# Sums of weight blocks made in DRAM during the first layer's down product, and a later turn of the last group

## The reference

```
for l in range(2):
    x = x + mixers(rms_norm(x)) @ w_out[l]            # even layer: convolution + differential attention
    h = rms_norm(x, ffn_norm_w[l])                    # odd layer: gated DeltaNet + forgetting attention
    x = x + (silu(h @ w_gate[l]) * (h @ w_up[l])) @ w_down[l]
return rms_norm(x, final_norm_w)
```

## Time and profile before

| | |
|---|---|
| median of 3 runs | 1217.36 us (1217.2 to 1217.74) |
| the profiled execution | 1218.75 us |
| its span, first to last instruction | 1216.9 us |
| busy: TensorE, DVE, ACT, POOL | 1201.6, 784.4, 566.3, 107.1 us |
| accumulating DMAs (POOL's queue q0) | 6912 packets, 24.38 MB |

### The profile page before, as it was taken

How to read it: one execution, slowest core, us unless ns; L and a number is a source line. 1 busy time by engine, 2 the same in 40 slices (tenths; PEclk the granted TensorE clock), 3 DMA queues, 4 the chain that set the end, 5 groups by cost and what they waited for, 6 DMA issues and landing times.

```text
span 1216.9 us, 16112 instructions
## 1 busy us (share of the span) xinstructions
PE 1201.6 (99%) x5831; PEld 972.4 (80%) x5831; DVE 784.4 (64%) x1233; ACT 566.3 (47%) x917; POOL 107.1 (9%) x209
## 2 busy tenths in 40 slices
PE   9999999999999999999999999999999999999998
PEld 7876648888888878888888788788888888888876
DVE  6787886786667763337677666545665455456796
ACT  6354455655555543325585254444243232324564
POOL 0000000011110100000002814400000000000120
PEclk9999999999999999999999999999999999999999
DMA  6243311687867533331322211022244443336881
GB/s 247 90 118 91 106 54 52 225 189 174 210 174 187 108 100 91 100 104 55 119 87 70 87 35 53 18 61 66 83 134 116 116 109 104 93 104 223 167 147 70
DMA packets 56643, 138.04 MB, mean 113 GB/s; under 512 B 21890, under 2 KB 22146, under 8 KB 56322
## 3 DMA queue, kind: packets, MB, share of 16 engines
q1 hardware_dynamic: 48754, 111.44, 28.7%
q0 software_dynamic: 6912, 24.38, 11.4%
q10 hardware_dynamic: 912, 1.35, 0.4%
HBM read 128.61 MB, written 2.10 MB: 107 GB/s over the span
## 4 chain that ended last, share of the span: by engine, by line
PE 89%; DVE 5%; ACT 3%; issue 1%; DMA 1%; ACTq 0%; SPq 0%; DVEq 0%
PE PS L2168 87%; PE PS L2481 1%; DVE wring L1648 1%; DMA raw<-w_stream 1%; PE PS L2244 1%; DVE resid L1652 0%; DVE kept L1688 0%; DVE cacc L1843 0%; ACT wring L924 0%; ACTq L1194 0%; DVE wring L1698 0%; PE PS L2559 0%; DVE AA L1692 0%; DVE out L2159 0%; DVE amax L1761 0%
## 5 line engine op out<-in xcount | busy, mean ns | idle before, releaser
L2168 PE MATMUL PS<-HH,wring 128*128 128x512 f32 x2136 | 506.2, 393 | 0.9 <-DVE vd L2094 0.9
L2168 PEld LDWEIGHTS PS<-HH,wring 128*128 128x128 f32 x2136 | 395.2, 188 | 81.4 <-issue 1.3
L2168 PE MATMUL PS<-wring,HH 128*128 128x512 f32 x672 | 156.0, 390 | 0.3 <-ACT wring L1139 0.3
L2168 PEld LDWEIGHTS PS<-wring,HH 128*128 128x128 f32 x672 | 125.7, 188 | 26.6 <-issue 0.6
L1698 DVE TENSOR_TENSOR wring<-raw,wring 128x1024 fp32r<-128x1024 f32 x91 | 111.8, 1231 | 48.2 <-ACT wring L924 48.1
L924 ACT ACTIVATE wring<-raw 128x1024 fp32r<-128x1024 f32 x91 | 95.8, 1056 | 96.0 <-PE PS L2168 68.6
L2168 PE MATMUL PS<-AS,wring 128*128 128x512 f32 x528 | 120.4, 389 | 0.0
L2168 PEld LDWEIGHTS PS<-AS,wring 128*128 128x128 f32 x528 | 99.0, 188 | 20.5
L2168 PE MATMUL PS<-wring,AA 128*128 128x512 f32 x462 | 105.4, 389 | 1.6 <-DVE wring L1648 0.8
L2168 PEld LDWEIGHTS PS<-wring,AA 128*128 128x128 f32 x462 | 86.6, 188 | 20.3 <-issue 2.3
L1464 DVE TENSOR_TENSOR ubuf<-PS,rstd 128x512 f32<-128x512 f32 x22 | 15.2, 690 | 83.9 <-PE PS L2168 83.9
(11 more groups left out here) (367 smaller groups left out, 1606.1 us busy)
## 6 DMA issues: line engine op xcount, KB each, us to landing
raw<-w_stream SPq DMA_DIRECT2D x131, 512.0 KB, 3.5
x_even<-w_glu POOLq DMA_DIRECT2D x12, 512.0 KB, 6.3
raw<-w_glu SPq DMA_DIRECT2D x10, 512.0 KB, 9.4
y_part<-w_glu SPq DMA_DIRECT2D x10, 512.0 KB, 6.6
w_part<-w_glu SPq DMA_DIRECT2D x10, 512.0 KB, 5.3
w_part<-w_glu POOLq DMA_DIRECT2D x10, 512.0 KB, 10.9
kept<-w_last POOLq DMA_DIRECT2D x10, 512.0 KB, 8.3
x_odd<-w_glu POOLq DMA_DIRECT2D x8, 512.0 KB, 6.2
```

Source lines behind the costliest of these rows:

```text
L2168: return nc.tensor.matmul(out, lhsT, rhs, start=start, stop=stop, skip_group_check=adds)
```

## The change

```diff
+MADE_OF = {P_21: 0, P_SUM: 1, P_ALL: 2, P_LAST: 3}
+SUM_HALVES = 2
...
+    GROWN_BEFORE = [16 * len(range(n, GROWN_0, ADDING)) for n in range(ADDING)]
...
-        return more_tile(i) if a in (P_22, P_LAST) else kept_tile(i)
+        return more_tile(i) if a in (P_22, P_SUM, P_LAST) else kept_tile(i)
...
@@ SP, the last product
-        sp.dma_start(more_first[:], last_d[B22][:, 0:3 * TILE]).then_inc(first_loaded[0], 16)
-        sp.wait_ge(sem("ffn_lo"), SPLITS_0 + HALF)
-        sp.wait_ge(sem("lhs_made"), MADE)
-        sp.dma_start(more_last[:], last_d[B22][:, 3 * TILE:HALF * S]).then_inc(first_loaded[1], 16)
+        for i in range(PIECES):
+            if i == 3:
+                sp.wait_ge(sem("ffn_lo"), SPLITS_0 + HALF)
+                sp.wait_ge(sem("lhs_made"), MADE)
+            sp.dma_start(more_tile(i), last_d[B22][:, columns_of(i)]).then_inc(more_loaded[i], 16)
+        for a in (P_21, P_SUM, P_ALL, P_LAST):
+            if a == P_LAST:
+                sp.wait_ge(added[SUM_HALVES], GROWN_BEFORE[SUM_HALVES] + 32)
+            else:
+                for h in range(SUM_HALVES):
+                    sp.wait_ge(added[h], GROWN_BEFORE[h] + 16 * sums_in_dram(a))
+            for i in range(PIECES):
+                free = last_tile((a - 2) * PIECES + i)
+                sp.wait_ge(lo_ready[free % RING], slot_round(free))
+                if a in (P_21, P_ALL):
+                    sp.dma_start(kept_tile(i), sums_d[MADE_OF[a]][:, columns_of(i)]).then_inc(kept_loaded[i], 16)
+                else:
+                    sp.dma_start(more_tile(i), sums_d[MADE_OF[a]][:, columns_of(i)]).then_inc(more_loaded[i], 16)
@@ POOL, behind the accumulations of layer 0
+        pool.wait_ge(tile_used, T_DN0 + RING)
+
+        def grow(n, step, to, addend, columns, adds):
+
+            if step or GROWN_BEFORE[n]:
+                pool.wait_ge(added[n], GROWN_BEFORE[n] + 16 * step)
+            if adds:
+                nc.gpsimd.dma_start(to[:, columns], addend[:, columns], accum_op=ALU.add, max_dma_last_dim=5632).then_inc(added[n], 16)
+            else:
+                nc.gpsimd.dma_start(to[:, columns], addend[:, columns]).then_inc(added[n], 16)
+
+        first, second, third, fourth = sums_d[0], sums_d[1], sums_d[2], sums_d[3]
+        every = slice(0, HALF * S)
+        chain = ((first, last_d[B11], False), (first, last_d[B21], True), (second, first, False), (second, last_d[B22], True),
+                 (third, second, False), (third, last_d[B12], True))
+        for step, (to, addend, adds) in enumerate(chain):
+            for h in range(SUM_HALVES):
+                grow(h, step, to, addend, slice(h * HALF * S // 2, (h + 1) * HALF * S // 2), adds)
+            if step < 2:
+                grow(SUM_HALVES, step, fourth, last_d[(B21, B22)[step]], every, step == 1)
         pool.wait_ge(evacuated, E_IN1)
         nc.gpsimd.memset(cin[:, 0:GTAPS - 1], 0.0).then_inc(sem("cin_zero"), 1)
...
-        for a, part, behind in ((P_21, B21, P_11), (P_LAST, B21, P_21), (P_ALL, B12, P_SUM)):
-            for i in range(PIECES):
-                add_to_kept(a, i, part, behind)
@@ DVE, last_product
-                if g // PIECES == P_21:
-                    i = g % PIECES
-                    dve.wait_ge(first_loaded[i // 3], 32)
-                    dve.wait_ge(lo_ready[last_tile(g) % RING], slot_round(last_tile(g)))
-                    V.tensor_tensor(kept_tile(i), kept_tile(i), more_tile(i), ALU.add).then_inc(sem("lhs_made"), 1)
@@ TensorE, down
+            pe.wait_ge(sem("copied"), 4 * GROUPED)
+            columns(4, range(RING))
+            pe.wait_ge(sem("ffn_mul"), glu_made(GROUPED - 1, "gate_first", 1))
+            columns(0, (0, 1))
+            turn_results(GROUPED - 1, 0)
+            columns(0, (2, 3))
+            pe.wait_ge(sem("ffn_mul"), glu_made(GROUPED - 1, "up_second", 1))
+            columns(2, (0, 1))
+            turn_results(GROUPED - 1, 2)
+            columns(2, (2, 3))
+            pe.wait_ge(sem("glu_kept"), 4 * GROUPED)
+            columns(6, range(RING))
```

More of the change, by code:

```diff
@@ L75 @@
 PRODUCT_BANK = (BANK_12, BANK_21, BANK_12, BANK_21, BANK_SUM, BANK_22, BANK_SUM)
-ADDED = (P_21, P_LAST, P_ALL)
+MADE_OF = {P_21: 0, P_SUM: 1, P_ALL: 2, P_LAST: 3}
+SUM_HALVES = 2
+SUM_STEPS = 6
 ADDING = 3
@@ L341, in shape_constants, with build @@
     return const, rope
-def build(nc, x_d, w_d, glu_d, last_d, vec_d, row_d, const_d, rope_d, final_d, out_d):
+def build(nc, sums_d, x_d, w_d, glu_d, last_d, vec_d, row_d, const_d, rope_d, final_d, out_d):
     f32, f32r, i32, bf16 = mybir.dt.float32, mybir.dt.float32r, mybir.dt.int32, mybir.dt.bfloat16
@@ L624, in build @@
     X_PART = (0, 1, 2, 3, 4, 4, 5, 5)
-    first_loaded = [sem(f"first_loaded{n}") for n in range(FIRST - RAW)]
+    more_loaded = [sem(f"more_loaded{n}") for n in range(PIECES)]
+    first_loaded = more_loaded[0:FIRST - RAW]
     gdn_mm, gdn_act, gdn_dve, gdn_pool = [[sem(f"gdn{n}_{e}") for n in range(2)] for e in ("products", "act", "dve", "pool")]
-    half_loaded = [sem(f"half_loaded{t}") for t in range(HALVED)]
+    half_loaded = more_loaded[FIRST - RAW:FIRST - RAW + HALVED]
     half_hi, half_lo = sem("half_hi"), sem("half_lo")
@@ L655, in product_done, with sums_in_dram, more_count, kept_count @@
             engine.wait_ge(tile_used, last_tile(a * PIECES + PIECES - 1) + 1)
-    def added_count(a, i):
-        return 16 * ((GROWN_0 + ADDED.index(a) * PIECES + i) // ADDING + 1)
+    def sums_in_dram(a):
+        return {P_21: 2, P_SUM: 4, P_ALL: 6}[a]
+    def more_count(a, i):
+        return 16 * ((1 if i < FIRST - RAW + HALVED else 0) + (P_22, P_SUM, P_LAST).index(a) + 1)
+    def kept_count(a):
+        return LOADED_0 + 16 * ((P_11, P_21, P_ALL).index(a) + 1)
+    GROWN_BEFORE = [16 * len(range(n, GROWN_0, ADDING)) for n in range(ADDING)]
     MADE = SUMS_0 + 3 * HALF
@@ L1081, in last_hi @@
                 act.wait_ge(raw_loaded[t % RAW], raw_count(t))
[L1082 to L1087, removed]
+            elif a in (P_11, P_21, P_ALL):
+                act.wait_ge(kept_loaded[i], kept_count(a))
             else:
-                act.wait_ge(added[(GROWN_0 + i) % ADDING], added_count(a, i))
+                act.wait_ge(more_loaded[i], more_count(a, i))
             act.wait_ge(tile_used, t - RING + 1)
@@ L1278, in _ @@
             if e == 8:
-                act.wait_ge(sem("l2_ms"), 1)
+                act.wait_ge(sem("gate_args"), 3)
                 nc.scalar.activation(l2s[:], l2s[:], ACT.Sqrt).then_inc(sem("l2_root"), 1)
@@ L1983, in _ @@
                 dve.wait_ge(sem("key_sums"), H)
-                V.tensor_scalar(l2s[:], l2s[:], 1e-6, None, ALU.add).then_inc(sem("l2_ms"), 1)
+                V.tensor_scalar(l2s[:], l2s[:], 1e-6, None, ALU.add).then_inc(sem("gate_args"), 1)
             if e == 8:
@@ L2503, in down, with columns @@
         def down(td):
[L2505 to L2516, removed]
+            def columns(first, ks):
+                for k in ks:
                     if first == 4:
@@ L2910 @@
     out = nc.dram_tensor("out_t", (NB, P, D), f32, kind="ExternalOutput").ap()
-    build(nc, *args, out)
+    sums = nc.dram_tensor("w_sums", (4, P, HALF * S), f32, kind="Internal").ap()
+    build(nc, sums, *args, out)
     r = run_bass_kernel_spmd(nc, [arrays], core_ids=[0])
```

## The result

The changed kernel takes 1237.95 us (1236.67 to 1238.21, 4 runs) against 1217.55 us (1217.2 to 1217.83) before: a ratio of 1.0163 with a 95% interval of 1.0150 to 1.0176, so it is slower by 1.6%. That is 0.7 us from the forecast of 1237.3, but the trace shows that the time came about in another way.

The account below looks back on a forecast made before the run. TensorE was taken as the bound, busy 1201.6 of 1216.9 us. Gains of 3.1 us and 23 us of POOL lateness on 1218.75 made 1238.6, less 1.4 for the profiled run: 1237.3 us, range 1213.5 to 1264.

Parts of the forecast that it names:

- The turn: In down, turning the last group after twelve more matmuls removes TensorE's wait at L2481: -1.5 us.
- the last product: Plain SP loads replace six DVE sums and 18 accumulating POOL DMAs, removing two TensorE waits: -1.56 us.
- The chain: POOL's fourteen DRAM-to-DRAM DMAs beside down: 104 us (bounds 78 and 131), making POOL 23 us late to the cin memset.
- the stream keeping its 27%: Down's load stream, 104 GB/s over 470 to 581 us, takes 27% of the DMA engines, leaving the chain 81 us.
- the 111 us: Room for the chain, from its start after down's fourth tile (470.5) until DVE needs POOL's memset (581.8).
- The dependence of TensorE on POOL's memset: At layer 1's start, each microsecond POOL reaches the cin memset behind 581.8 costs TensorE one.
- 154 that I took: GB/s assumed for the chain's DRAM additions, from the row for accumulations alone: 56 us for three additions.
- The rival "the stream starves": In down, tiles land later than 8.6 us several times running beside the chain; costs 5 to 10 us; chance 0.13.
- The fourth sum's copy: Chain copy with rows of 22 KB, beside which the stream would need more tiles than otherwise; no size given.
- The rule of the Trainium skill: DMA engines take queues in turn, a whole packet each; basis for the stream rival's 7.4 us per tile beside copies.
- The Trainium skill's remark that packets are preferably at most 4 KB: If long rows were cut so, the stream would get half of the packets and its starvation rival would cost nothing.
- The Trainium skill's 214 GB/s for copies between HBM tensors: Alternative rate for the chain's copies: 54 us instead of 48, POOL late by 29 us, time 1243.

Follow-up runs that it names:

- late_one: Changed kernel with POOL's chain moved behind POOL's last operation for layer 1, long rows, one transfer of 1408 KB in flight: 1214.44 us, ratio 0.9972.
- early_one: Changed kernel with POOL's chain in its place, but one transfer of 1408 KB in flight and rows limited to 2816 bytes: 1258.29 us.
- fourth_rows: Changed kernel with only the copy for the fourth sum limited to rows of 5632 bytes: 1233.79 us.
- the three runs on rows: Changed kernel with shorter rows in the chain's copies, in copies and additions, or in the fourth sum's copy only: 1226.72, 1222.48 and 1233.79 us.
- rows_short: Changed kernel with the chain's copies limited to 2816 (packets of 5,632 bytes in the trace), same bytes and order: 1226.72 us.
- rows_all_short: Changed kernel with the limit of 2816 in both the chain's copies and its additions: 1222.48 us.
- early_one_dve: Changed kernel with the chain in its place, one transfer in flight, limit 2816, and cin cleared by DVE instead of POOL: 1214.90 us, ratio 0.9982.
- late: Changed kernel with POOL's chain, rows and all, moved behind POOL's last operation for layer 1: 1223.58 us, ratio 1.0043.
- late_paced: Changed kernel with the chain behind POOL's last operation for layer 1, in four quarters by columns, rows of 2816 bytes, one transfer in flight: 1213.60 us, ratio 0.9964.
- no_chain: Changed kernel without POOL's chain, the last product loading single blocks instead of sums (result left wrong): 1213.88 us, ratio 0.9969.

## Why the prediction was right in number and wrong in cause

*The turn, the last product* (-1.5 and -1.56): right, -1.8 and -2.0 measured by medians, with the named rows gone.

*The chain: 104 us of work, the stream keeping its 27%, POOL late by 23 us.* This step failed, and in its premise. I priced the sharing as if the stream took what it needs and the chain the rest. The stream had no such precedence: the chain moved its 20.2 MB to step 4 in 96.5 us, 209 GB/s, inside the 111 us, while the stream, with its tiles 9 and 11 us apart at the worst, fell behind TensorE. POOL was not late at all. The 104 us were also too long for this chain, which took 96.5 us beside the stream. That isn't because each transfer was faster than I took it: by the first copy and the first addition of late_one, one at a time (6.5 and 13.0 us for a half), the same four copies and three additions would take 130 us (an estimate: 8 x 6.5 + 6 x 13.0). Two and three in flight overlap, which I had not priced.

*The dependence of TensorE on POOL's memset, one microsecond for one*: right, as early_one shows, but not in play.

*The rival "the stream starves"*: this is what happened, and it was mis-sized. Its place, its long rows and its condition (landing later than 8.6 us several times in a row) hold: the tiles at 480.55, 491.40 and 497.34 landed some 11, 18 and 14 us after they were asked for. Its price was 5 to 10 us and is 22.6. Missing were the late feed of layer 1 behind the late tiles in ACT's and DVE's queues (6.3 us of gaps), and what TensorE loses behind gaps (6.8 us: the lower clock behind the two long ones, and the new starts). The fourth sum's copy, whose rows of 22 KB I named in a bracket and did not price, has packets of 45 KB; fourth_rows puts 4.2 us on them. The rule of the Trainium skill that I set beside it (DMA: Bandwidth & Descriptors, "Queues, rings and completion order") agrees with the 17.9 us by turns against the 17.7 measured, and in its direction with the three runs on rows: shorter rows of the one queue give the other more. The Trainium skill's remark that packets are preferably at most 4 KB (same page, "SWDGE vs HWDGE vs iDMA") gives no protection here: the trace has packets of 11 and 45 KB, and rows_short, which cuts them, is 11.2 us faster.

*The Trainium skill's 214 GB/s for copies between HBM tensors*: in late_one the first copy of 1408 KB takes 6.5 us from issue to the next issue (778.46 to 784.96), 222 GB/s with its latency in it; two later ones take 6.9 and 8.8 us. The first addition takes 13.0 us (784.96 to 797.94), 111 GB/s, less than the 154 that I took.

That forecast and result agree within 0.1% is chance: 23 us of one mechanism replaced 22.6 of another.

What stays open: why layer 1's first tiles still land late beside two transfers in flight in short rows (rows_all_short), and in time beside one (early_one_dve). The pauses between transfers are one reason that the shares suggest (0.85 in late_one against 0.99 in late); the number of packets that wait at each engine is another, and no run here separates them.

## What to carry to other kernels

A background transfer isn't served after the stream that feeds the bound engine but beside it, so price it by what it leaves the stream per tile, not by the idle share of the DMA engines, and read the packets' sizes from the trace, not from the program. Give it short rows and, above all, one transfer in flight: late_paced is 4.3 us faster than the kernel before and has the lowest median, 1213.60 us, though the intervals of late_one, early_one_dve and no_chain overlap with its own. Look at where the stream's tiles share an in-order queue with the next stage's feed: that is where a late load costs last. And look at what stands behind such a chain in the issuing engine's queue: one memset was worth 43 us in early_one.

## What the runs showed of the hardware that I had not expected

Copies and additions from DRAM to DRAM ran beside the stream at 298 GB/s in total over 470 to 566 us of the changed kernel. The copy of a whole block went in packets of 45 KB, of 2.06 us each, and beside them the stream got 91 packets of 4 KB for 97 of POOL's. A limit of 2816 made packets of 5,632 bytes in copies and of 2,816 in additions. Cutting the copies' packets from 11 and 45 KB to 5.6 KB made the chain 1.8 us longer in 98. And a gap of 3.3 us was followed by nine at a mean granted clock of 0.81; with the new starts, the stalls cost 43% more than their gaps show (6.8 beside 15.8 us).
